# A grouped-expert decoder kernel: an earlier gate matrix, and a gather that leaves out padding rows

## The chip, the cores and the metric

The kernel runs on one core of one Trainium2 chip. The metric is the device time of one execution in microseconds (us), as the median of the runs. The engines are named as in the profile: PE is TensorE (PEld its weight loads), DVE is VectorE, ACT is ScalarE, POOL is GpSimd, SP is the engine that issues most DMAs. L671 is line 671 of the kernel.

## The reference

Two decoder layers over 512 tokens of width 1024, all in float32. Each layer has a mixer (sliding-window attention and a chunked mLSTM, gated, summed, one output projection) and then a grouped mixture of experts, which is where the change acts:

```python
h2 = rms_norm(x, norm_ffn_w[l]) * (1.0 + sc2) + sh2
x = x + g2 * grouped_moe(h2, router_w, router_bias, w_gate[l], w_up[l], w_down[l])
...
# grouped_moe: best of 4 groups, then the top 2 of its 4 experts; 16 experts in all
order = jnp.argsort(flat_e)
...
x_pad = jnp.zeros((n_blocks * MOE_BLOCK, D), xt.dtype).at[dest].set(xt[tok_sorted])
...
return (jax.nn.silu(xb @ w_gate[e]) * (xb @ w_up[e])) @ w_down[e]
```

Every token goes to two experts, so a layer has 1024 rows to work on. An expert has a gate and an up matrix of 1024x512 and a down matrix of 512x1024, 2 MB each. How many rows of the blocks below are real follows from the inputs; counted with the reference's router, 64 rows to a block, they are:

| layer | real rows of its blocks, in order | blocks |
|---|---|---|
| first | 64, 25, 64, 4, 47, 64, 38, 45, 64, 8, 54, 47, 64, 32, 63, 56, 63, 64, 8, 38, 63, 49 | 0 to 21 |
| second | 50, 34, 46, 52, 52, 64, 6, 64, 26, 64, 2, 64, 64, 10, 64, 13, 64, 16, 64, 39, 52, 23, 33, 58 | 0 to 23 |

## The kernel before, in words

The kernel is written engine by engine, with semaphores by hand. One loop over the two layers stands in each engine's program, and the order of the work is the order of the lines.

**The expert stage.** The 1024 rows are sorted by expert and cut into blocks of 64 rows; an expert's last block is filled up with padding rows. For each block PE transposes the 64 gathered rows (`x_transposes`, L1324), DVE and ACT scale them into feature layout (L1934, L920), PE multiplies them by the gate and up matrices (`gate_up`, L1332, 32 matmuls), ACT applies silu (L925), DVE multiplies the two halves (L1984, the product), PE transposes the hidden rows (L1338), ACT copies them (L928) and PE multiplies by the down matrix (`down`, L1344, 16 matmuls). The loop is software pipelined: in one pass PE runs the gate/up group of block b+1, the row transposes of block b+2, the down group of block b and the hidden-row transposes of block b+1. The loop's first pass is preceded by `x_transposes(0)`, `gate_up(0)`, `x_transposes(1)` and `h_transposes(0)`.

**Where the rows come from.** ACT stores the normalised token rows to a DRAM buffer, `token_rows` (L912). Block 0 is not gathered; it is picked on PE by one-hot matmuls (L1319, semaphore `first_rows`) and copied into the buffer `xg[0]` by ACT and DVE (L916, L1923). All later blocks are gathered by an indirect DMA that POOL issues (`gather_rows`, L671) into `xg[0]` or `xg[1]` in turn; these are the upper and lower 64 partitions of the first 1024 columns of `merged`, which the mixer's output projection read before. The list of token numbers, `idx`, is made on DVE and PE: one-hot matrices of row in block, block, and token tile (L1920 to L1929), a matmul that sums them (L1368), and two DVE instructions that join tile and row to a token number (L1941, L1942). A padding row finds no token, so its sum is 0 and it gathers token 0. POOL issues the gather for block 1 as soon as `idx` is there, and the gather for block b+2 when the transposes of block b are done. The loop also issues one gather past the last block.

**Where the weights lie and when they are loaded.** There are three buffers for each of gate, up and down; expert e uses buffer e mod 3. All loads go through SP, in this order before the expert loop: the gate matrix of expert 1 (L554), up 0 (L557), down 0 and down 1 (L559, L560), gate 0 (L562), then after the output projection up 1 and down 2 (L564, L565), then gate 2 (L567) and up 2 (L570). Gate 2 goes into `hT`, the mixer's feature buffer. The mixer's last matmul from it is over before L559, but its first two 512-column slices also serve as the place where ACT writes squares that nobody reads (`squares`, L146; L906, only the row sums count); so SP waits for the four square passes (`ffn_sq`, L566) before it loads gate 2. Up 2 goes into `regA`, where the normalised rows lie until block 0 is picked and the rows are stored; so SP waits for `first_rows` and `rows_out` (L568, L569). Then SP issues the small parameter loads of the next layer (first layer only), waits until all engines have reached the expert stage, clears the mixer's semaphores, and loads each further expert when its buffers come free: gate and up behind the last gate/up group of expert e-3, down behind its last down group (`load_expert`).

**What else lies on the path.** On POOL the lines before the first gather are L674 to L676: the wait for the cleared semaphores, for the stored rows, and for `idx`. `vaug` is the mLSTM's value buffer, 2064 columns wide and free in the expert stage; its first 1024 columns hold a quarter of the second expert's down matrix.

## Time and profile before

| | us |
|---|---|
| runs, median (three: 1625.84, 1629.93, 1628.45) | 1628.45 |
| the profiled execution | 1632.27 |
| its span, first to last instruction | 1630.5 |
| PE busy in it | 1525.3 |
| DVE busy | 671.4 |
| ACT busy | 325.2 |
| POOL busy | 127.6 |

The profiled execution is 3.82 us above the median of the runs, and 1.77 us of it lie around the span. How to read the rows further below: a page's chain gives the shares of the span along the chain of work that ended last. The chain in order of time gives start, length and what it was. A timeline row gives start, length, engine, line, operation, output<-input, shape and count, and in brackets how long the engine was idle before it and what ended that. A row by stretch gives from:to, its length, the busy time of PE, PEld, DVE, ACT and POOL with instructions in brackets, the granted TensorE clock as a share of full speed, the busy share of the DMA engines and GB/s.

### The profile page before, as it was taken

Reading aid. Unit: us, or ns where it says so; the run is one execution under the profiler, and the core shown is the slowest. Engines: PE = TensorE matmul, PEld = TensorE weight load, DVE = VectorE, ACT = ScalarE, POOL = GpSimd, SP = SyncE. Lnnn points to the kernel's source line nnn. Section 1 sums busy time; section 2 is a strip of 40 time slices with the busy share of each in tenths; the row PEclk is TensorE's granted clock in tenths of the full one; section 3 lists DMA queues with packets and bytes.
Section 4 is the critical chain, followed back from the end, with each engine's and each line's share of the span. In section 5 each row is a group of like instructions: output and inputs, shape, how many; then the busy total and the mean of one; then the engine's idle time right before and its main releaser. Section 6 shows DMA issues by size and latency. Waiting matters only on the chain.

```text
span 1630.5 us, 19269 instructions
## 1 busy us (share of the span) xinstructions
PE 1525.3 (94%) x6035; PEld 690.6 (42%) x6036; DVE 671.4 (41%) x1670; ACT 325.2 (20%) x836; POOL 127.6 (8%) x197
## 2 busy tenths in 40 slices
PE   5999999989998899989889999999899988999996
PEld 2644445544454333323354444454444533333332
DVE  1446425557625322211345554365673351212224
ACT  3234411100001212111143342111000111212120
POOL 1100000001000010100110000000100010101001
PEclk9999999999999999999999999999999999999998
DMA  9961112377726799999954012126765389997895
GB/s 337 347 243 52 52 52 100 107 258 268 282 81 244 219 354 389 390 387 393 346 193 176 1 52 103 52 103 210 288 225 218 107 315 390 392 383 254 317 346 200
DMA packets 131893, 376.10 MB, mean 231 GB/s; under 512 B 12232, under 2 KB 14448, under 8 KB 131824
## 3 DMA queue, kind: packets, MB, share of 16 engines
q1 hardware_dynamic: 117440, 337.51, 55.9%
q0 software_dynamic: 5984, 20.45, 4.0%
q10 hardware_dynamic: 8400, 17.31, 2.8%
q8 instruction: 33, 0.54, 0.1%
q14 instruction: 36, 0.29, 0.1%
HBM read 345.36 MB, written 29.88 MB: 230 GB/s over the span
## 4 chain that ended last, share of the span: by engine, by line
PE 80%; DMA 7%; DVE 5%; ACT 2%; issue 2%; SPq 1%; another core or an unknown queue 1%; POOL 0%; DVEq 0%; ACTq 0%; POOLq 0%
PE bank L1085 25%; PE bank L1332 17%; PE bank L1074 11%; PE bank L1344 8%; PE bank L1290 7%; DMA weight_ring<-in_w_up_dram 3%; DMA regA<-in_w_up_dram 2%; PE bank L1324 2%; DMA h_features<-in_ada_w_dram 1%; DMA merged_features<-token_rows,regU 1%; PE bank L1154 1%; PE bank L1338 1%; PE bank L1143 1%; DVE x_tokens L2033 1%
## 5 line engine op out<-in xcount | busy, mean ns | idle before, releaser
L1085 PE MATMUL bank<-h_features,weight_ring 128*128 128x512 f32 x768 | 344.0, 602 | 1.9 <-ACT regB L800 1.9
L1332 PE MATMUL bank<-weight_ring,merged_features 128*64 128x512 f32 x960 | 222.5, 618 | 14.8 <-DMA weight_ring<-in_w_up_dram 8.7
L1085 PEld LDWEIGHTS bank<-h_features,weight_ring 128*128 128x128 f32 x768 | 146.4, 193 | 183.3 <-issue 183.0
L1074 PE MATMUL bank<-weight_ring,h_features 128*128 128x512 f32 (+1 forms) x512 | 196.8, 541 | 5.0 <-ACT merged_features L760 3.8
L1984 DVE TENSOR_TENSOR merged_features<-bank,merged_features 64x512 f32<-64x512 f32 x46 | 31.9, 693 | 350.6 <-ACT merged_features L925 345.8
L1074 PEld LDWEIGHTS bank<-weight_ring,h_features 128*128 128x128 f32 x512 | 95.7, 190 | 99.4 <-issue 94.7
L1332 PEld LDWEIGHTS bank<-weight_ring,merged_features 128*64 128x64 f32 x960 | 73.0, 142 | 140.4 <-issue 136.6
L1344 PE MATMUL bank<-weight_ring,merged_features 128*64 128x512 f32 x528 | 122.3, 605 | 4.9 <-ACT merged_features L928 4.9
L1332 PE MATMUL bank<-h_features,merged_features 128*64 128x512 f32 x256 | 117.3, 612 | 8.0 <-DMA regA<-in_w_up_dram 6.9
L1290 PE MATMUL bank<-weight_ring,merged_features 128*128 128x512 f32 x256 | 116.3, 610 | 3.0 <-POOL merged_features L664 3.0
L1332 PE MATMUL bank<-regA,merged_features 128*64 128x512 f32 x256 | 117.7, 614 | 0.0
L925 ACT ACTIVATE merged_features<-bank 64x512 f32<-64x512 f32 x46 | 27.1, 589 | 330.2 <-PE bank L1332 330.2
L1290 PEld LDWEIGHTS bank<-weight_ring,merged_features 128*128 128x128 f32 x256 | 48.8, 195 | 59.9 <-issue 56.7
L1981 DVE TENSOR_TENSOR merged_features<-bank,g_rows 128x512 f32<-128x512 f32 x46 | 31.8, 691 | 86.2 <-PE bank L1344 82.5
L1332 PEld LDWEIGHTS bank<-h_features,merged_features 128*64 128x64 f32 x256 | 34.8, 141 | 70.8 <-issue 70.8
L920 ACT ACTIVATE merged_features<-bank,mod_cols,scale 128x64 f32<-128x64 f32 x192 | 62.0, 403 | 9.3 <-PE bank L1324 7.1
L1344 PEld LDWEIGHTS bank<-weight_ring,merged_features 128*64 128x64 f32 x528 | 35.9, 138 | 64.6 <-issue 62.5
L1085 PE MATMUL bank<-regB,weight_ring 128*128 128x512 f32 x128 | 57.9, 595 | 1.6 <-DVE regB L1784 1.6
L1085 PE MATMUL bank<-regA,weight_ring 128*128 128x512 f32 x128 | 57.7, 594 | 0.0
L1934 DVE TENSOR_SCALAR merged_features<-bank,scale,mod_cols 128x64 f32<-128x64 f32 x192 | 52.8, 336 | 4.2 <-PE bank L1324 2.0
L671 POOL DMA_INDIRECT merged_features<-token_rows,regU x46 | 43.9, 953 | 66.4 <-DVEq L1943 31.8
L642 POOL TENSOR_TENSOR fin_small<-fin_small,minus_half 128x4 f32<-128x4 f32 x8 | 8.1, 1007 | 509.3 <-DVEq L1533 509.3
(363 smaller groups left out, 1567.3 us busy)
## 6 DMA issues: line engine op xcount, KB each, us to landing
weight_ring<-in_w_gate_dram SPq DMA_DIRECT2D x22, 2048.0 KB
weight_ring<-in_w_up_dram SPq DMA_DIRECT2D x22, 2048.0 KB
weight_ring<-in_w_down_dram SPq DMA_DIRECT2D x22, 2048.0 KB, 16.6
weight_ring<-in_w_in_dram SPq DMA_DIRECT2D x18, 2048.0 KB, 13.7
x_tokens<-in_ada_w_dram SPq DMA_DIRECT2D x14, 2048.0 KB, 8.0
h_features<-in_w_gate_dram SPq DMA_DIRECT2D x10, 2048.0 KB
regA<-in_w_up_dram SPq DMA_DIRECT2D x10, 2048.0 KB
regA<-in_ada_w_dram SPq DMA_DIRECT2D x8, 2048.0 KB, 8.3
```

The lines of the kernel that those rows point to most:

```text
L671: po.indirect_dma_start(out=xg[p], out_offset=None, in_=xlin, in_offset=bass.IndirectOffsetOnAxis(ap=index, axis=0)).then_inc(xg_in[p], 16)
L920: last = ac.activation(xT[:, k, :], ps[2][:, MB * k:MB * k + MB], ACT.Identity, scale=A2[:, k:k + 1], bias=modc[:, 24 + k:25 + k])
L925: ac.activation(hsil[64:P, :], ps[3][0:64, :], ACT.Silu).then_inc(sil_ready, 1)
L1074: ins = te.matmul(bank[:, 0:w], hT[:, k, P * i:P * i + P], wv[:, k, :], start=(k == 0), stop=(k == KD - 1))
L1085: ins = te.matmul(bank[:, :], wv[:, k, c0:c0 + P], rhs[:, k, :], start=(k == 0), stop=(k == kn - 1))
L1290: ins = te.matmul(bank[:, :], merged[:, k, P * i:P * i + P], slot(f"wo{k // 4}", 4, D)[:, k % 4, 512 * h:512 * h + 512], start=(k == 0), s ...
L1324: ins = te.transpose(ps[(2, 6)[k % 2]][:, MB * k:MB * k + MB], xg[p][:, P * k:P * k + P], ident[MB * p:MB * p + MB, MB * p:MB * p + MB])
L1332: ins = te.matmul(ps[3][64 * part:64 * part + 64, :], xT[:, k, :], w[:, k, :], start=(k == 0), stop=(k == KD - 1))
L1344: ins = te.matmul(ps[5][64 * half:64 * half + 64, :], hxT[:, k, :], down_w[p][k][:, 512 * half:512 * half + 512], start=(k == 0), stop=(k ...
L1934: last = ve.tensor_scalar(xT[:, k, :], ps[6][:, MB * k:MB * k + MB], A2[:, k:k + 1], modc[:, 24 + k:25 + k], ALU.mult, ALU.add)
L1981: ve.tensor_tensor(to, ps[5][:, :], g2bc[:, :], ALU.mult).then_inc(y_taken, 1)
L1984: ve.tensor_tensor(hx, ps[3][64:P, :], hsil[64:P, :], ALU.mult).then_inc(hx_ready, 1)
```

## The change

It has two parts. SP issues the gate matrix of the third expert (expert 2) ahead of the first down matrices and no longer waits for the square passes; for that, the squares' scratch moves from `hT` to columns 1024 to 2047 of `vaug`. And the list of token numbers is shifted so that a padding row gets 1024 where it got 0: the tile number is counted from -8 (`iog` holds -8 to -5) and 8 x 128 = 1024 is added again at the end, so that a real row's number comes out as before while a row without a token keeps 1024. The gather gets a bound of 511 and leaves out rows beyond it without an error. A left-out row keeps what its buffer held; therefore POOL clears `xg[1]` once per layer, behind the wait for the first expert's rows.

```diff
--- before.py
+++ after.py
@@ -143,7 +143,6 @@
         gate_parts = regU[:, 519:519 + S]
         mflat = merged[:, :, :].rearrange("p a b -> p (a b)")
         small = mflat[:, 0:D]
-        squares = hT[:, 0:2, :].rearrange("p a b -> p (a b)")
         head_squares = mflat[:, 1024:2048]
 
         xg = [mflat[0:MB, 0:D], mflat[MB:2 * MB, 0:D]]
@@ -160,6 +159,7 @@
 
         zeros = vaug[:, :, :, :].rearrange("p a b c -> p (a b c)")[:, 0:D]
         vflat = vaug[:, :, :, :].rearrange("p a b c -> p (a b c)")
+        squares = vflat[:, D:2 * D]
         yg = [[regB[:, D * i:D * i + D] for i in range(NT - 1)] + [vflat[:, 0:D]], [xn[:, i, :] for i in range(NT)]]
 
         as8 = lambda ap: ap.rearrange("p (k n) -> p k n", k=KD)
@@ -303,6 +303,7 @@
         lg_taken = lsem("lg_taken")
         first_picked, first_rows, first_low, first_high = (lsem(n) for n in (
             "first_picked", "first_rows", "first_low", "first_high"))
+        rows_empty = lsem("rows_empty")
         z_there, inverse, idx_sum, idx_there = (lsem(n) for n in ("z_there", "inverse", "idx_sum", "idx_there"))
         routed, tables, combined = lsem("routed"), lsem("tables"), esem("combined")
         xt_ready, xt_evac_a, xt_evac_d, gu_ready, sil_ready, hx_ready, ht_ready, ht_evac, y_ready, y_taken = (
@@ -556,6 +557,7 @@
                 through(sp, "gb", 7)
                 load_up(0, 0)
                 through(sp, "yb", 7)
+                load_gate(2, 2)
                 load_down(0, 0)
                 load_down(1, 1)
                 summed(sp, len(STREAM) - 1)
@@ -563,8 +565,6 @@
                 through(sp, "wo", 2 * NT - 1)
                 load_up(1, 1)
                 load_down(2, 2)
-                sp.wait_ge(ffn_sq, NT)
-                load_gate(2, 2)
                 sp.wait_ge(first_rows, 1)
                 wait_reg(sp, rows_out, l * (16 * NT) + 16 * NT)
                 load_up(2, 2)
@@ -669,8 +669,12 @@
                 def gather_rows(p, index):
 
                     po.indirect_dma_start(out=xg[p], out_offset=None, in_=xlin,
-                                          in_offset=bass.IndirectOffsetOnAxis(ap=index, axis=0)).then_inc(xg_in[p], 16)
-
+                                          in_offset=bass.IndirectOffsetOnAxis(ap=index, axis=0),
+                                          bounds_check=S - 1, oob_is_err=False).then_inc(xg_in[p], 16)
+
+                pool.wait_ge(first_rows, 1)
+                po.memset(xg[1], 0.0).then_inc(rows_empty, 1)
+                pool.wait_ge(rows_empty, 1)
                 wait_reg(pool, moe_cleared, l + 1)
                 wait_reg(pool, rows_out, l * (16 * NT) + 16 * NT)
                 pool.wait_ge(idx_there, 1)
@@ -1925,7 +1929,7 @@
                 link(ve.tensor_tensor(at_block, io64[:, 0:32].unsqueeze(1).to_broadcast([P, 2 * NT, 32]),
                                       block.unsqueeze(2).to_broadcast([P, 2 * NT, 32]), ALU.is_equal))
                 link(ve.tensor_tensor(at_tile.rearrange("p (k i) b -> p k i b", k=2), at_block.rearrange("p (k i) b -> p k i b", k=2),
-                                      io64[:, 0:NT].unsqueeze(1).unsqueeze(3).to_broadcast([P, 2, NT, 32]), ALU.mult))
+                                      iog[:, :].unsqueeze(1).unsqueeze(3).to_broadcast([P, 2, NT, 32]), ALU.mult))
                 link(ve.tensor_scalar(at_block, at_block, pcol[:, 0:1], None, ALU.mult))
                 ve.sem_inc(inverse, 1)
 
@@ -1938,7 +1942,7 @@
                 dve.wait_ge(xt_ready, 1)
                 xt_dve()
                 dve.wait_ge(idx_sum, 1)
-                link(ve.tensor_copy(r(800, 32)[0:MB], ps[7][0:MB, P:P + 32]))
+                link(ve.tensor_scalar(r(800, 32)[0:MB], ps[7][0:MB, P:P + 32], 8.0 * P, None, ALU.add))
                 link(ve.scalar_tensor_tensor(idx[:, :], ps[7][0:MB, P + 32:P + 64], float(P), r(800, 32)[0:MB], ALU.mult, ALU.add))
                 ve.sem_inc(idx_there, 1)
 
```

## Rows read from the trace of the kernel before

**Rows 1.** The page's chain that ended last, whole span, by engine.

```profile
PE 80%; DMA 7%; DVE 5%; ACT 2%; issue 2%; SPq 1%; another core or an unknown queue 1%; POOL 0%; DVEq 0%; ACTq 0%; POOLq 0%
```

**Rows 2.** The chain in order of time: start, length, what it was.

```profile
523.67 8.84 DMA merged_features<-token_rows,regU
...
549.90 7.06 PE bank L1332 x32
...
706.53 27.39 DMA weight_ring<-in_w_up_dram
...
758.10 28.37 DMA weight_ring<-in_w_up_dram
...
1312.04 8.95 DMA merged_features<-token_rows,regU
...
1352.56 26.07 DMA regA<-in_w_up_dram
```

**Rows 3.** Engines, granted clock and DMA by stretch.

```profile
460.00:503.00 43.00, 42.21 (x148) 20.41 (x147) 11.35 (x20) 4.64 (x9) 1.11 (x2) 1.00 0.06 25
507.00:527.00 20.00, 15.96 (x109) 9.29 (x111) 15.66 (x70) 2.50 (x8) 2.06 (x2) 1.00 1.01 395
...
535.00:543.00 8.00, 7.72 (x24) 2.60 (x26) 5.11 (x22) 0.00 (x0) 0.71 (x1) 0.61 0.38 105
...
586.00:786.00 200.00, 189.82 (x958) 70.28 (x952) 39.73 (x96) 36.21 (x96) 16.57 (x30) 0.97 1.03 388
1339.00:1376.00 37.00, 34.66 (x180) 12.82 (x176) 7.46 (x18) 6.79 (x18) 3.33 (x6) 1.00 1.01 379
```

**Rows 4.** SP's queue: issues of gate 2, up 2, and down 3 in the second layer.

```profile
506.64 0.37 SPq L520 DMA_DIRECT2D h_features<-in_w_gate_dram  x1
519.96 0.37 SPq L523 DMA_DIRECT2D regA<-in_w_up_dram  x1
...
1338.33 0.37 SPq L527 DMA_DIRECT2D weight_ring<-in_w_down_dram  x1
```

**Rows 5.** The gather's line in 500 to 586, 586 to 786, and 1339 to 1376.

```profile
DMA to landing us min/median/max: 3.7/4.5/8.8
...
L671 POOL DMA_INDIRECT merged_features<-token_rows,regU x15: 927/927/930, 594.0 to 768.9; - x15
...
DMA to landing us min/median/max: 6.8/6.9/7.1
...
L671 POOL DMA_INDIRECT merged_features<-token_rows,regU x3: 932/932/935, 1347.9 to 1371.1; - x3
```

**Rows 6.** The timeline around the first gather of both layers.

```profile
523.67 1.51 POOL L671 DMA_INDIRECT merged_features<-token_rows,regU  x1 [15.93 <-DVEq L1943]
...
531.83 0.69 DVE L1984 TENSOR_TENSOR merged_features<-bank,merged_features 64x512 f32<-64x512 f32 x1 [2.54 <-issue]
...
532.64 0.49 PE L1324 MATMUL bank<-ident,merged_features 64*128 64x64 f32 x5 [2.45 <-DMA merged_features<-token_rows,regU]
532.91 0.27 PE L1338 MATMUL bank<-ident,merged_features 64*128 64x64 f32 x1
...
535.28 10.01 PE L1332 MATMUL bank<-weight_ring,merged_features 128*64 128x512 f32 x32 [1.91 <-ACT merged_features L920]
...
1319.95 0.69 DVE L1984 TENSOR_TENSOR merged_features<-bank,merged_features 64x512 f32<-64x512 f32 x1 [2.27 <-remote]
1321.13 0.49 PE L1324 MATMUL bank<-ident,merged_features 64*128 64x64 f32 x5 [2.55 <-DMA merged_features<-token_rows,regU]
...
1324.07 9.86 PE L1332 MATMUL bank<-weight_ring,merged_features 128*64 128x512 f32 x32 [2.20 <-ACT merged_features L920]
```

**Rows 7.** A memset on POOL, and two instructions of VectorE.

```profile
L613 POOL MEMSET mlstm_v_and_one<- 128x1024 f32 x1 | 0.9, 950 | 0.0
...
L1563 DVE TENSOR_SCALAR regP<-x_tokens,c_padded x8: 477/1531/1535, 344.9 to 1203.2; 128x512 f32<-128x512 f32 x8
...
520.36 0.41 DVE L1925 TENSOR_TENSOR regU<-iota,regP 128x256 bf16<-128x256 f32 x1
```

## The prediction, made before the changed kernel was run

> **What bounds the kernel now.** I read the page's chain first, then the chain in order of time, then the timeline around the two places where the change acts, then the DMA share by stretch.
>
> The chain [rows 1] names TensorE for 80% of the span and DMA for 7%. So a saving counts only where one of the few DMA links of that chain gets shorter, or where TensorE's own work moves closer together. The chain in time [rows 2] has these links. In each layer, TensorE waits once for the gather of the second block of expert rows (8.84 and 8.95 us from the issue on POOL to the landing). In the first layer it later waits twice for an up matrix that landed 27.39 and 28.37 us after its issue, the second time at the last expert; in the second layer once, 26.07 us after issue. A 2 MB matrix needs some 5.4 us at 388 GB/s, so those loads stood in a queue for most of that time. The stretches confirm it [rows 3]: from 586 to 786 us all DMA engines are busy (share 1.03, 388 GB/s), from 1339 to 1376 as well (1.01, 379 GB/s). From 460 to 503 us DMA is nearly idle (0.06), from 507 to 527 it is full (1.01).
>
> So there are two kinds of time to win: bytes that leave the two full stretches, and the wait for the first gather.
>
> **The gate matrix of the third expert.** Today it is issued at 506.64 and the up matrix of the same expert at 519.96 [rows 4], behind the up and down matrices of experts 1 and 2. The change issues the gate ahead of the first down matrices, before the idle stretch that begins at 460 [rows 3], so its 2 MB push the loads behind it back by some 5.4 us into that stretch. Those loads are first used once the first expert's rows are there, not before 519 us, so nothing waits for them. No DMA is added, and SP loses one wait. What it wins: TensorE waits for no weights in the next 180 us (the first such link of the chain is issued at 706.53 [rows 2]), so the earlier landing itself is worth 0. What it can help is the first gather, which today is issued (523.67) while up22, as I call the third expert's up matrix, is still queued behind the gate. up22 cannot be issued earlier (it overwrites the normalised rows), but it now meets an empty queue and ends near 526 (519.96 + 5.4), while today it is the last of a queue that is full to beyond 527 [rows 3]. In the first expert blocks a gather lands after 3.7 us at best, 4.5 in the middle and 8.8 for this one [rows 5]; I take 5 to 6.5 us, a landing 2.3 to 3.8 us earlier, before the first gate/up group ends at 530.19 (the 2.45 us of idle before 532.64 [rows 6]).
>
> How much of that reaches the end? In the first layer, the transposes of the gathered rows start at 532.64, and the transposes of the hidden rows at 532.91, right behind [rows 6]. The latter wait for VectorE's product, which starts at 531.83 after 2.54 us of its own issue (no data was late) and takes 0.69, so it ends at 532.52. That is what is late next: the wait moves from the gather to this product. The second gate/up group starts at 535.28, 2.4 us after the hidden-row transposes. Bounds for the gain: 0.1 us if that 2.4 us is TensorE's own queue (loop entry, expert numbers, branches), 1.0 us if it is only the scaling of the gathered rows, which VectorE could then start at 532.5. In the second layer the product ends at 1320.64, 0.5 us before the transposes start at 1321.13; there the bounds are 0.5 and 1.4. Both layers have nearly the same distance between the transposes and the next group (2.64 us from 532.64, 2.94 from 1321.13) and the same code, so I take the low ends: **0.15 and 0.5 us**.
>
> **The padding rows.** The reference's router gives 22 and 24 blocks of 64 rows, and each layer also gathers one block more than it has, all padding. In the full stretch of the first layer lie 15 gathers (issued 594.0 to 768.9 [rows 5]): blocks 8 to 21 and the empty one. Padding in them: 0, 56, 10, 17, 0, 32, 1, 8, 1, 0, 56, 26, 1, 15 and 64 rows, 287 in all. A padding row today is a 4 KB read like any other: the 15 land within 6.8 to 7.1 us, the empty one among them [rows 5]. Left out, they are 1.18 MB less; at 388 GB/s, **3.0 us**, and since the queue never runs dry there, the last expert's up matrix lands that much earlier and the layer ends that much earlier. In the full stretch of the second layer lie three gathers [rows 5], blocks 5, 6 and 7, with 0, 58 and 0 padding rows: 0.24 MB at 379 GB/s, **0.6 us**. Elsewhere the queue has idle time and the rows are worth 0. Bounds: 0 if a left-out row still costs a transfer, 3.6 if it costs none; I take 3.6, as a read that is not issued leaves the queue.
>
> **What is added.** One POOL memset of 64x1024 per layer, behind the wait for the first expert's rows and ahead of the first gather on POOL. A 128x1024 one took 0.95 us [rows 7]. Those rows are there just before 519.96, when SP issues up22 behind the same wait [rows 4], and POOL then idles until the gather at 523.67 [rows 6], so the memset is hidden with nearly 3 us to spare; without that cover each layer would lose 0.95. But it runs beside VectorE's index work, which lies on the path. The 128x512 VectorE scaling takes 0.477 us at its fastest and 1.53 as a rule [rows 7], so something holds it. I bound the price by 0 and 0.95 per layer; begun at about 519.8 the memset would still run for 0.35 us when L1925 is due (520.36 [rows 7]), and I take **0.35 us per layer**. The Trainium skill (GPSIMD Engine Reference, 8. Key points) says that GpSimd shares its SBUF interfaces with VectorE, with contention for instructions in a 2-port mode or with two SBUF inputs: L1925 would be one of these, and the full rule would give the upper bound, a sum of 2.4 instead of 3.6. The 1.53 us agrees with it; no row shows a memset beside VectorE.
>
> The index arithmetic keeps its instruction count and shapes, the scratch of the squares only changes its buffer: 0. The bounded gather has no row: its POOL time is bounded by 0.93 (today, median of the loop) below and, as nothing in the trace prices a check, left open above; in the loop it is covered by two blocks of matmuls.
>
> **Sum:** 0.15 + 0.5 + 3.0 + 0.6 - 2 x 0.35 = 3.55 us, taken as 3.6. The profiled execution took 1632.27 us (span 1630.5); it would take 1628.7. The median of the runs is 1628.45, 3.8 us lower, and all differences are local, so I predict 1628.45 - 3.6 = **1624.9**.
>
> **Rivals.** *A, the gap closes (faster).* If VectorE's scaling and not TensorE's queue sets the second group, it starts 1.0 and 1.4 us earlier. Its 32 matmuls now take 10.01 and 9.86 us against 7.06 a block later [rows 2, 6]: after the idle time the granted clock falls to its lower level of 1.2 GHz (mean 0.61 from 535 to 543 [rows 3]). A shorter gap may keep it at 2.4 GHz, worth 2.95 us in the first layer. In the second layer little of it counts: the down matrix of the fourth expert, issued at 1338.33 [rows 4], starts the full stretch, and the queue has only about 0.5 us of slack before it, which the 0.5 has used. Time: 1624.9 - 0.85 - 2.95 = 1621.1. For it: idle time there shrinks. Against it: the pause for VectorE's product remains.
> *B, left-out rows are not free.* If the descriptors are still made and drained, or the queue's share goes to nobody who is waited for, the 3.6 us stay: 1628.5. For it: nothing but that no row shows a skipped read.
> *C, slower: the bounded gather is slow on POOL.* The place is the first gather of each layer. It lands now at 532.50, and after the queue's relief there are some 3 us in hand before it sets the transposes again. At 0.1 us per row, 6.4 us more, it would be 3.4 us late in both layers: 1624.9 + 6.8 = 1631.7. From about 0.17 us per row one gather would outlast a block (15 in 174.9 us [rows 5], 12.5 us apart) and pace the whole loop. Against it: 0.93 us for 64 rows today is 15 ns per row.
>
> **Chances.** Forecast 0.62, A 0.20, B 0.11, C 0.07. No change means within 0.3% (4.9 us, 1623.6 to 1633.3), about what a measurement can tell. The forecast lies within it; a tenth of the chance, from its upper side, is beyond. Faster 0.20 + 0.10 = 0.30; slower 0.05 (C beyond 1633.3); the rest, 0.65, the same. The range takes in the forecast with its bounds, nearly all of A, and B: 1620.3 to 1629.4; C lies outside.
>
> **What would show it.** Right: no idle time of TensorE named for the first gather; VectorE's product named in its place before the second group; some 4.1 MB less on the software queue; the last up matrix of the first layer lands 3 us earlier relative to the start of its expert stage. Wrong: the gather landing is unchanged (then the queue ahead was not its delay); the second group runs in 7 us (A); the 15 gathers still land after 7 us and the full stretch is as long (B); POOL's gather instruction is several us long (C).

## The result, and the profile after

The changed kernel takes **1619.06 us** (median of 10 runs); beside it, on the same chip, the kernel before took 1625.96 (median of 10). The ratio is 0.995 with a 95% interval of 0.9937 to 0.9962: 6.9 us by the medians. Forecast were 1624.9 us and a gain of 3.6, so the time lies just below the range (1620.3). Part of the distance is the base: the three runs that the forecast started from had a median of 1628.45, ten have 1625.96. Timed again with the experiments, the change had a ratio of 0.9933 (0.9916 to 0.9951). So the gain is 7 to 10 us, two to three times the forecast.

Most lines of the changed kernel stand four below those of the kernel before (L1332 is now L1336); the gather is still L671.

The chain that ended last names DMA for 4% of the span, where it was 7% [rows 1]:

```profile
PE 82%; DVE 5%; DMA 4%; SPq 3%; ACT 3%; issue 2%; POOL 0%; DVEq 0%; ACTq 0%; POOLq 0%
```

The chain in order of time has no gather left in it, and the last up matrices land 26.14 and 23.29 us after their issue instead of 28.37 and 26.07 [rows 2]:

```profile
534.90 1.11 DVE merged_features L1938 x4
536.01 1.48 issue
537.49 7.09 PE bank L1336 x32
...
756.11 26.14 DMA weight_ring<-in_w_up_dram
...
1351.07 23.29 DMA regA<-in_w_up_dram
```

The timeline around the first gather of the first layer, answering to [rows 4, 6, 7] (the bracket at the end of a row is the engine's idle time and what ended it): SP issues the early gate matrix at 439.74 and the up matrix of the same expert at 521.59; the memset runs beside VectorE; TensorE starts the transposes of the gathered rows without a wait, and then waits for VectorE's product.

```profile
439.74 0.38 SPq L521 DMA_DIRECT2D h_features<-in_w_gate_dram  x1
...
521.40 0.95 POOL L676 MEMSET merged_features<- 64x1024 f32 x1 [12.03 <-PE bank L1323]
521.59 0.37 SPq L524 DMA_DIRECT2D regA<-in_w_up_dram  x1
521.99 0.41 DVE L1929 TENSOR_TENSOR regU<-iota,regP 128x256 bf16<-128x256 f32 x1
...
533.45 0.71 PE L1328 MATMUL bank<-ident,merged_features 64*128 64x64 f32 x8
534.17 0.69 DVE L1988 TENSOR_TENSOR merged_features<-bank,merged_features 64x512 f32<-64x512 f32 x1 [3.32 <-ACT merged_features L929]
535.01 0.43 PE L1342 MATMUL bank<-ident,merged_features 64*128 64x64 f32 x4 [0.86 <-DVE merged_features L1988]
```

The same two stretches of full DMA as in [rows 3]; the columns are busy time of PE, PEld, DVE, ACT and POOL with their instructions, then granted clock, DMA share, GB/s. The engines of the DMA are as busy as before, but move 391 and 390 GB/s instead of 388 and 379:

```profile
586.00:786.00 200.00, 189.90 (x964) 71.39 (x962) 39.75 (x96) 36.30 (x96) 17.16 (x30) 0.98 1.03 391
1339.00:1376.00 37.00, 34.69 (x180) 12.84 (x178) 7.46 (x18) 6.80 (x18) 3.44 (x6) 0.99 1.02 390
```

**How much of the two spans may be compared.** The span fell from 1630.5 to 1619.6, more than the medians. At the end of the second layer of the first profile stand two waits whose releaser the trace does not name:

```profile
1605.04 0.69 DVE L1981 TENSOR_TENSOR merged_features<-bank,g_rows 128x512 f32<-128x512 f32 x1 [3.53 <-remote]
1607.86 0.38 ACT L928 ACTIVATE merged_features<-bank 128x256 f32<-128x256 f32 x1 [6.88 <-remote]
```

They cost that execution 5.6 us (21.84 us from the last gate/up group to the matmuls of the kept rows); in all the 15 other profiles of this study, the unchanged kernel's second one among them, that stretch takes 16.24 us. It belongs to one execution and to neither kernel. The parts ahead of the experts, which the change hardly touches, also differ from profile to profile, by some 7 us, with the places where the granted clock falls. So the experiments are read by stretches that begin and end inside the expert stage:

- **S1**: from the gate/up group of block 15 to that of the last block in the first layer. It holds the second half of the first full DMA stretch, and its end is set by the last up matrix.
- **S2**: in the second layer, from SP's issue of the fourth expert's down matrix to the gate/up group of the sixth expert, which waits for an up matrix; **G** is how long that group then runs.

All from the timelines, in us; the time is the ratio to the kernel before in the same series, with its interval.

| kernel | ratio | S1 | S2 | G |
|---|---|---|---|---|
| before, first profile | | 84.78 | 40.44 | 9.82 |
| before, again | 0.9997 (0.9984 to 1.001) | 84.54 | 42.30 | 9.91 |
| early gate alone | 0.9985 (0.9971 to 1.0) | 84.35 | 40.43 | 9.69 |
| early gate alone, again | 0.9994 (0.998 to 1.0009) | 84.32 | 40.56 | 9.05 |
| the change, no row left out | 0.9977 (0.9964 to 0.999) | 84.88 | 40.40 | 9.20 |
| before, padding reads 64 rows | 1.0017 (1.0003 to 1.0032) | 84.49 | 40.36 | 9.64 |
| left out in blocks 1 to 7 | 0.9968 (0.9953 to 0.9982) | 84.29 | 38.85 | 8.78 |
| left out from block 8 on | 0.9963 (0.9949 to 0.9978) | 81.82 | 40.78 | 9.47 |
| left out in block 6 | one run | 85.06 | 37.63 | 8.78 |
| left out in blocks 9, 13, 18, 22 | one run | 81.68 | 40.54 | 9.51 |
| left out in blocks 8 to 21 but these | one run | 85.14 | 40.38 | 9.65 |
| rows left out, gate as before | 0.9932 (0.9913 to 0.995) | 81.21 | 37.88 | 8.78 |
| the same without memset | 0.9943 (0.9921 to 0.9964) | 81.40 | 37.88 | 8.78 |
| the change | 0.995 (0.9937 to 0.9962) | 81.27 | 37.64 | 8.78 |
| the change, again | 0.9933 (0.9916 to 0.9951) | 81.49 | 38.44 | 8.78 |
| the change without memset | 0.9939 (0.992 to 0.9959) | 81.54 | 37.48 | 8.78 |

(42.30 in the second line: there the fourth down matrix was issued 2.3 us earlier after the first pick than in the first profile, behind a queue that had not drained: the DMA engines were busy, at 405 GB/s, in the last 1 us before the issue, and moved 127 GB/s there in the first profile.)

### The profile page after: what moved, and what is told of

Its sections match the earlier page's. It is cut to its first block, busy times and chain, and to the rows that moved or that the text cites. A ratio compares the mean times of both kernels' runs of the same rounds, so it can differ in the third digit from the quotient of the medians.

```text
span 1619.6 us, 19319 instructions
## 1 busy us (share of the span) xinstructions
PE 1523.4 (94%) x6035; PEld 691.9 (43%) x6036; DVE 671.6 (41%) x1670; ACT 326.1 (20%) x836; POOL 131.6 (8%) x199
## 2 busy tenths in 40 slices
DMA packets 131893, 371.97 MB, mean 230 GB/s; under 512 B 13242, under 2 KB 15458, under 8 KB 131824
## 3 DMA queue, kind: packets, MB, share of 16 engines
q0 software_dynamic: 5984, 16.32, 3.2%
## 4 chain that ended last, share of the span: by engine, by line
PE 82%; DVE 5%; DMA 4%; SPq 3%; ACT 3%; issue 2%; POOL 0%; DVEq 0%; ACTq 0%; POOLq 0%
PE bank L1089 26%; PE bank L1336 18%; PE bank L1078 12%; PE bank L1348 8%; PE bank L1294 7%; DMA weight_ring<-in_w_up_dram 2%; PE bank L1328 2%; DMA regA<-in_w_up_dram 1%; DMA h_features<-in_ada_w_dram 1%; PE bank L1342 1%; PE bank L1158 1%; PE bank L1147 1%; DVE x_tokens L2037 1%; SPq L524 1%; DVE regP L1569 1%
## 5 line engine op out<-in xcount | busy, mean ns | idle before, releaser
L1336 PE MATMUL bank<-weight_ring,merged_features 128*64 128x512 f32 x960 | 222.0, 616 | 15.2 <-DMA weight_ring<-in_w_up_dram 8.9
L1336 PEld LDWEIGHTS bank<-weight_ring,merged_features 128*64 128x64 f32 x960 | 73.2, 141 | 140.2 <-issue 136.4
L1336 PE MATMUL bank<-h_features,merged_features 128*64 128x512 f32 x256 | 114.5, 601 | 4.2 <-DMA regA<-in_w_up_dram 3.2
L1336 PE MATMUL bank<-regA,merged_features 128*64 128x512 f32 x256 | 115.0, 603 | 0.0
L1336 PEld LDWEIGHTS bank<-h_features,merged_features 128*64 128x64 f32 x256 | 34.1, 138 | 64.6 <-issue 64.6
L671 POOL DMA_INDIRECT merged_features<-token_rows,regU x46 | 44.9, 976 | 44.3 <-POOL regU L688 19.5
```

Source lines behind the costliest of these rows:

```text
L671: po.indirect_dma_start(out=xg[p], out_offset=None, in_=xlin, in_offset=bass.IndirectOffsetOnAxis(ap=index, axis=0), bounds_check=S - 1, o ...
L1336: ins = te.matmul(ps[3][64 * part:64 * part + 64, :], xT[:, k, :], w[:, k, :], start=(k == 0), stop=(k == KD - 1))
```

## The experiments

**The two parts, each alone.** Rows alone, as an edit of the change (the scratch of the squares goes back to `hT` as well):

```diff
                 through(sp, "yb", 7)
-                load_gate(2, 2)
                 load_down(0, 0)
...
                 load_down(2, 2)
+                sp.wait_ge(ffn_sq, NT)
+                load_gate(2, 2)
```

> The part on padding rows alone: gate matrix of the third expert and the scratch of the squares as before; index 1024, bounded gather and memset as in the change. Theory (the bytes pay): most of the change's 6.9 us is here: 1620 to 1622 us, the last up matrix of the first layer lands 3 to 4 us earlier after the first pick than before, while TensorE still waits for the first gather, as it stands behind the same queue. Rival (the gate pays, by an earlier second gate/up group that keeps the clock): within 2 us of the kernel before, 1624 to 1627. Rival (the code after the expert loop): the two waits for an unknown releaser behind the last expert (6.88 and 3.53 us in the second layer) are there or not whatever the edit.

Gate alone, as an edit of the change (the two index operations are as before, too):

```diff
-                                          in_offset=bass.IndirectOffsetOnAxis(ap=index, axis=0),
-                                          bounds_check=S - 1, oob_is_err=False).then_inc(xg_in[p], 16)
+                                          in_offset=bass.IndirectOffsetOnAxis(ap=index, axis=0)).then_inc(xg_in[p], 16)
...
-                pool.wait_ge(first_rows, 1)
-                po.memset(xg[1], 0.0).then_inc(rows_empty, 1)
-                pool.wait_ge(rows_empty, 1)
```

> The early gate matrix alone: its load ahead of the first down matrices and the squares in the other scratch; gather without bound, padding index 0, no memset. Theory (the bytes pay): 1623.5 to 1625.5, the first gather lands 2 to 4 us earlier, the full stretch is as long as before. Rival (the gate pays): 1619 to 1621, the second gate/up group of the first layer runs in about 7.1 us instead of 10.

Measured: rows alone 1615.75 us against 1626.85, more than was expected of them; gate alone 1623.86, ratio 0.9985, inside what was expected if the bytes pay. Leaving out the rows shortens S1 and S2, the gate neither. The gate does what it was meant to do for the queue, but less than forecast: the up matrix of the third expert meets an idle queue and still lands 8.2 to 8.3 us after its issue in the first layer, and the first gather 7.67 us after its own (7.04 in the second profile, 8.84 before). In the first layer of the first of these profiles TensorE still waits for that gather:

```profile
537.64 0.68 PE L1323 MATMUL bank<-ident,merged_features 64*128 64x64 f32 x8 [1.28 <-DMA merged_features<-token_rows,regU]
```

The second rival fails: with the gate alone the second gate/up group of the first layer took 8.58 us, not 7.1.

**The kernel before, again.**

> The kernel before, unchanged, profiled again. If the waits for an unknown releaser behind the last expert belong to that program, they come back with 6.9 and 3.5 us within 0.5; if they are luck of one execution, they are shorter or gone, and the profiled span is some 4 to 6 us shorter than 1630.5. The time is that of the kernel before within 0.1%.

1625.83 us, span 1623.6; the two unnamed waits are gone. They were luck of one execution, and none of the change's gain.

**The bound without its effect** (padding index 0, everything else as in the change):

```diff
-                                      iog[:, :].unsqueeze(1).unsqueeze(3).to_broadcast([P, 2, NT, 32]), ALU.mult))
+                                      io64[:, 0:NT].unsqueeze(1).unsqueeze(3).to_broadcast([P, 2, NT, 32]), ALU.mult))
...
-                link(ve.tensor_scalar(r(800, 32)[0:MB], ps[7][0:MB, P:P + 32], 8.0 * P, None, ALU.add))
+                link(ve.tensor_copy(r(800, 32)[0:MB], ps[7][0:MB, P:P + 32]))
```

> The whole change but for the index: the two index operations on VectorE stay as before, so padding rows read row 0 again and the bound leaves none out; early gate, memset and bound check are in. It leaves out nothing of the result. Theory (the bytes pay): 1623.5 to 1625.5 as with the early gate alone, plus at most 0.7 for the memset. Rival (the bytes cost nothing, the rest pays): 1619 to 1620, as the whole change. The memset beside VectorE shows as a longer index operation, by at most 0.95 us a layer.

1624.17 us; S1 and S2 as before. Early gate, memset and bound check together are worth about as much as the gate alone. The last sentence of the expectation was wrong: L1929 took 0.41 us beside the memset, as it did without one [rows 7].

**One row read many times?** Before, all padding rows read row 0. This kernel reads 64 different rows instead, as many bytes:

```diff
+ link(ve.tensor_scalar(r(596, 1)[0:MB], pcol[0:MB, 0:1], -8.0, 8.0 * P, ALU.mult, ALU.add))
+ link(ve.tensor_scalar(r(564, 32)[0:MB], r(532, 32)[0:MB], 8.0 * P - 0.5, None, ALU.is_gt))
+ link(ve.tensor_scalar(r(564, 32)[0:MB], r(564, 32)[0:MB], r(596, 1)[0:MB], None, ALU.mult))
+ link(ve.tensor_tensor(idx[:, :], r(532, 32)[0:MB], r(564, 32)[0:MB], ALU.subtract))
```

> The kernel before, but a padding row r of a block reads token row 8r instead of row 0: as many bytes and packets as before, from 64 different rows. Four more tiny VectorE operations ahead of the first gather of a layer, some 0.7 us, of which the second gate/up group may wait for a part. Theory (the bytes pay): 1626 to 1628, not faster than before; in the second layer the up matrix of the sixth expert lands 40 to 41 us after the issue of the fourth down matrix, as before (40.4), and its 16 parts still lie 2 us apart from the median to the last. Rival (many reads of one row hold up one of the DMA engines, and the change wins by leaving that row alone): that landing comes after 38.5 to 39.5 us, with the last part within 1 us of the median, and the time falls by 2 us or more.

1629.01 us, S2 40.36: nothing is won by leaving row 0 alone. That rival falls. The time lies above the expected 1626 to 1628; the gap before the second gate/up group is 6.80 and 6.38 us there, behind the four added operations (5.09 and 5.49 before). One sign of the expectation was wrong: the 16 parts in which the matrix lands are 0.5 us apart from the middle one to the last, not 2. With the gate alone that distance is 2.0 in one profile and 0.8 in the other, with the last part at the same place, so it is no measure of the padding.

**Which blocks?** The index is shifted for some columns of the list only, one column to a block; the first of the two kernels:

```diff
+ link(ve.tensor_tensor(at_tile.rearrange("p (k i) b -> p k i b", k=2)[:, :, :, 0:8],
+                      at_block.rearrange("p (k i) b -> p k i b", k=2)[:, :, :, 0:8],
+                      iog[:, :].unsqueeze(1).unsqueeze(3).to_broadcast([P, 2, NT, 8]), ALU.mult))
+ link(ve.tensor_tensor(at_tile.rearrange("p (k i) b -> p k i b", k=2)[:, :, :, 8:32],
+                      at_block.rearrange("p (k i) b -> p k i b", k=2)[:, :, :, 8:32],
+                      io64[:, 0:NT].unsqueeze(1).unsqueeze(3).to_broadcast([P, 2, NT, 24]), ALU.mult))
...
+ link(ve.tensor_copy(r(800, 32)[0:MB], ps[7][0:MB, P:P + 32]))
+ link(ve.tensor_scalar(r(800, 32)[0:MB, 0:8], ps[7][0:MB, P + 0:P + 8], 8.0 * P, None, ALU.add))
```

> The whole change, but only the padding rows of blocks 1 to 7 get index 1024; those of later blocks read row 0 again. One or two more VectorE operations ahead of the first gather. Theory (bytes in the full stretches pay): the first layer's full stretch (blocks 8 to 21) is as long as before, 84.4 us from the gate/up group of block 15 to that of the last block; in the second layer the up matrix of the sixth expert lands 37.5 to 38 us after the issue of the fourth down matrix (40.4 before); 1621 to 1623 in all. Rival (the rows of the first layer are all that pays): both stretches as before, 1624.

> The counterpart: only the padding rows of blocks 8 and later are left out. Theory (bytes in the full stretches pay): 81.2 us from the gate/up group of block 15 to that of the last block in the first layer (84.5 before), 40.4 in the second layer as before; 1620 to 1622 in all. Rival (the gain comes from the few blocks of the second layer's start): 1624.

1621.82 and 1622.21 us. The first shortens S2 and leaves S1, the second S1 and leaves S2, so both layers pay, each through its own full stretch; either half is worth 4 to 5 us with the gate. S2 in the first, 38.85, is longer than the 37.5 to 38 that were expected; the experiment on block 6 alone shows why.

**The change again.**

> The change itself again, with a profile. Theory: 1617 to 1621; 81.2 us in the first layer's full stretch and 37.6 us to the up matrix of the sixth expert in the second, as in the first profile of it; the place and number of the low stretches of the granted clock differ, and so do the parts in front of the experts, by 2 or 3 us either way. If its stretches differ from the first profile of it by as much as from the kernel before, nothing can be read from single profiles.

1616.99 us, S1 81.49, S2 38.44: the stretches repeat within some 0.2 and 0.8 us.

**The memset, the gate, once more.** The change, and rows alone, without the memset, and the gate alone a second time:

```diff
-                pool.wait_ge(first_rows, 1)
-                po.memset(xg[1], 0.0).then_inc(rows_empty, 1)
-                pool.wait_ge(rows_empty, 1)
```

> The change without its memset and the two waits around it: rows that the first gather leaves out keep what the buffer held, finite numbers that no token reads. Theory (the memset's price is off the path: the first gather is issued 0.6 us later with it, but TensorE does not wait for that gather): the same as the change within 1 us, 1616 to 1619; first gather issued 7.6 us after the first pick's start instead of 8.2. Rival (0.35 to 0.6 us a layer are on the path): faster than the change by 0.7 to 1.2 us.

> The part on padding rows alone, without the memset: the gate matrix is loaded where it was before. Theory (left-out bytes carry the gain): 1615 to 1619, no slower than the change; 81.2 us from the gate/up group of block 15 to the last one in the first layer, 37.6 to 38.6 us from the issue of the fourth down matrix to the gate/up group of the sixth expert in the second. Rival (the early gate matrix carries 2 to 3 us of the change): 1619 to 1621.

> The early gate matrix alone, again, for a tighter interval: by the idle time that it takes out of the path (0.04 us in each layer in the first profile of it) the same as before within 0.1%; by its first timing 0.15% faster. TensorE names VectorE's product and not the gather ahead of the second gate/up group in both layers.

1616.26, 1617.93 and 1624.63 us (ratios 0.9939, 0.9943, 0.9994). The memset costs nothing that these runs can tell; the gate adds nothing where rows are left out (0.9932 and 0.9943 without it, 0.995, 0.9933 and 0.9939 with it). One reason in the expectation was wrong. The first gather is indeed issued 8.24 us after the first pick's start instead of 7.63, but it is so without the memset too. The index list is complete at 524.93 in the profile of the change (L1946 ends) and the gather starts at 525.91; before, these were 523.30 and 523.67. So the bounded form itself starts 0.6 us later, while the loop's gathers are hardly longer (0.967 us, 0.927 before [rows 5]).

**Block 6 alone.** The same edit with column 6 as the only shifted one (`[:, :, :, 6:7]`). The expectation set the engine time of 58 rows against a hold-up of the whole queue.

> The change with only block 6's padding rows left out: 58 in the second layer, 26 in the first. Theory (a left-out row is worth its engine time, some 0.24 us on one of 16 engines, 0.9 us for 58 rows): in the second layer 39.3 to 39.7 us from the issue of the fourth down matrix to the gate/up group of the sixth expert (40.4 with none left out, 38.9 with blocks 1 to 7). Rival (the gather of block 6 held the queue up as a whole): 38.9 or less. The first layer's full stretch as before, 84.4.

S2 is 37.63: **the whole gain of S2 comes from leaving out rows of this one gather**, 2.8 us where its 58 rows are 0.6 by their bytes. Here the theory of the forecast falls. The next two views say why. First, 4 us of the kernel before and of this one, both begun 3.5 us after the issue of block 6's gather (columns as above):

```profile
1362.90:1366.90 4.00, 4.00 (x22) 1.47 (x20) 0.00 (x0) 0.00 (x0) 0.00 (x0) 1.00 1.04 341
```

```profile
1360.50:1364.50 4.00, 4.00 (x22) 1.43 (x20) 0.00 (x0) 0.00 (x0) 0.00 (x0) 1.00 1.03 405
```

All 16 DMA engines are busy in both (1.04, 1.03), but while 64 rows are gathered they move 341 GB/s, and 405 while six are. The 4 us after such a gather show 416 GB/s or so; after block 5's, in the kernel before:

```profile
1354.80:1358.80 4.00, 4.00 (x26) 1.50 (x23) 0.64 (x1) 1.30 (x4) 0.18 (x1) 1.00 1.04 416
```

So a gather of 64 rows takes its 0.26 MB, 0.64 us at 410 GB/s, and on top of that (410 - 341) x 4 = 0.28 MB of what the queue would have moved, 0.67 us. Second, the queues over S2, the kernel before and the change (queue, packets, MB, share of 16 engines):

```profile
q1 hardware_dynamic: 3346, 13.24, 87.3%
q0 software_dynamic: 287, 0.91, 7.9%
```

```profile
q1 hardware_dynamic: 3286, 13.00, 89.5%
...
q0 software_dynamic: 220, 0.44, 4.1%
```

The gathers are q0. It falls by 0.47 MB, and block 6's padding is only 0.24 of them. The rest is the gather of block 7: before, it was issued at 1371.1 and its rows came ahead of the awaited up matrix (1378.63); now that matrix lands at 1374.36, 4.6 us after the gather's issue at 1369.7, and most of the rows come behind it. By these rates one emptied gather gives some 1.2 us, and that lets the next one slip behind the transfer that is waited for, up to another 1.3.

The profiles can be put in order by it. In the kernels that leave block 6 whole, all 64 rows of block 7 begin ahead of the sixth expert's group. With blocks 1 to 7 left out, 62 of them still do, and S2 is 38.85: the emptied gather by itself is worth 1.6 us. In the others that empty it, 47, 30, 28, 19, 14 and 8 rows do, and S2 is 38.44, 37.88, 37.88, 37.64, 37.63 and 37.48. So what the second step adds differs from execution to execution, 0.4 to 1.4 us; no run moved the gather of block 7 by itself.

**Does the same hold in the first layer?** There the forecast in bytes had come out right (3.0; S1 fell by 3.2). The four emptiest gathers of the full stretch alone, and the thinned ones alone; the first of the two kernels (the constant 1024 is added for the same columns):

```diff
+ link(ve.tensor_tensor(at_tile.rearrange("p (k i) b -> p k i b", k=2)[:, :, :, 0:32],
+                      at_block.rearrange("p (k i) b -> p k i b", k=2)[:, :, :, 0:32],
+                      io64[:, 0:NT].unsqueeze(1).unsqueeze(3).to_broadcast([P, 2, NT, 32]), ALU.mult))
+ link(ve.tensor_tensor(at_tile.rearrange("p (k i) b -> p k i b", k=2)[:, :, :, 9:14:4],
+                      at_block.rearrange("p (k i) b -> p k i b", k=2)[:, :, :, 9:14:4],
+                      iog[:, :].unsqueeze(1).unsqueeze(3).to_broadcast([P, 2, NT, 2]), ALU.mult))
+ link(ve.tensor_tensor(at_tile.rearrange("p (k i) b -> p k i b", k=2)[:, :, :, 18:23:4],
+                      at_block.rearrange("p (k i) b -> p k i b", k=2)[:, :, :, 18:23:4],
+                      iog[:, :].unsqueeze(1).unsqueeze(3).to_broadcast([P, 2, NT, 2]), ALU.mult))
```

> The change with padding rows left out in blocks 9, 13, 18 and 22 alone: 56, 32, 56 and 64 rows, 208 of the 287 in the first layer's full stretch. More small VectorE operations ahead of the first gather, which shift the start of the experts and not the stretch that is read. Theory D (a gather costs its bytes and, for some 4 us, a part of the rate of the whole queue, and only one that is mostly empty gives the rate back): the stretch from the gate/up group of block 15 to that of the last block as short as with all left out, 81.0 to 81.6 us. Theory B (each left-out row is worth 4 KB at 388 GB/s, 10.6 ns): 84.5 - 2.2 = 82.3.

> The counterpart: left out in blocks 8 to 21 but for 9, 13 and 18: 79 rows in eight gathers that keep 38 to 63 of their 64 rows. Theory D: nothing, 84.3 to 84.9 us. Theory B: 84.5 - 0.8 = 83.7.

81.68 and 85.14 us: theory D. The 208 rows of four gathers carry 2.9 of the 3.2 us, the 79 rows of eight others show no gain (one profile each; the kernels that leave out no row of S1 lie between 84.29 and 85.06). The same windows of 4 us in both, first the emptiest alone, for the gathers of blocks 17 (full), 18 (8 rows), 21 (full) and 22 (none):

```profile
709.80:713.80 4.00, 4.00 (x20) 1.41 (x18) 0.00 (x0) 0.00 (x0) 0.00 (x0) 1.00 1.03 345
721.40:725.40 4.00, 4.00 (x20) 1.55 (x18) 0.00 (x0) 0.00 (x0) 0.00 (x0) 1.00 1.03 395
...
765.10:769.10 4.00, 4.00 (x20) 1.36 (x18) 0.00 (x0) 0.00 (x0) 0.00 (x0) 1.00 1.03 334
776.70:780.70 4.00, 4.00 (x22) 1.70 (x20) 0.00 (x0) 0.00 (x0) 0.00 (x0) 1.00 1.03 404
```

then the thinned ones alone, for the gathers of blocks 18 (full), 19 (38 rows), 21 (49) and 22 (full):

```profile
720.10:724.10 4.00, 1.69 (x6) 0.83 (x8) 0.00 (x0) 0.00 (x0) 0.00 (x0) 0.84 1.03 334
736.80:740.80 4.00, 0.77 (x2) 0.33 (x4) 0.00 (x0) 0.00 (x0) 0.00 (x0) 0.89 1.03 346
766.00:770.00 4.00, 4.00 (x20) 1.35 (x18) 0.00 (x0) 0.00 (x0) 0.00 (x0) 1.00 1.04 324
777.60:781.60 4.00, 4.00 (x22) 1.70 (x20) 0.00 (x0) 0.00 (x0) 0.00 (x0) 1.00 1.03 342
```

A gather of 8 or no rows gives the rate back (395, 404), one of 49 runs at 324 although it moves a quarter less itself. All 16 profiles say the same. In the 4 us that begin 3.5 us after the issue, for blocks 8 to 22 of the first layer and 5 to 7 of the second, the engines move 334 GB/s in the mean (289 to 352) with 64 rows, 327 (291 to 349) with 38 to 56, 373 (364 to 380) with 32, and 392 (362 to 406) with 8 or fewer; in the next 4 us it is 414.

A rival to the rate is left in part. A matrix lands in 16 parts, and the wait ends with the last of them. For the last up matrix of the first layer the first and the last lie 0.5 to 0.7 us apart where no row of S1 is left out, 1.65 with the thinned gathers alone, 1.05 with the emptiest alone, and 2.2 to 2.5 with all of them. So leaving out rows brings the parts forward unequally, and the last one least. With the thinned gathers alone the middle part comes no earlier either (84.5 us from block 15's group, 83.8 to 84.3 in the six kernels that leave out nothing), so this is not the whole reason; the runs do not separate its share. (The times of these two, 1630.15 and 1631.1 in one run each, hold more VectorE work ahead of the first gather and are not used.)

## Why the prediction was wrong, step by step

**The gate matrix (0.15 + 0.5): the direction right, the relief smaller, the size not shown.** The up matrix behind the gate was to end 5.4 us after its issue and the gather to land after 5 to 6.5, before the first gate/up group ends. With the gate alone the matrix took 8.2 to 9.3 us, and the gather 7.67 and 7.04 in the first layer and 6.12 and 5.88 in the second. In the first layer of one of these profiles TensorE still waits for it for 1.28 us, and for 2.50 with the bound and the memset added. In the change it lands after 5.79 and 4.97, where rows of block 1 are left out too, and no idle time of TensorE is named for it. VectorE's product is what is late next, as forecast, though not for its own issue: in most profiles it waits for ACT's silu. From the end of the first gate/up group to the start of the second the first layer has 4.95 us with the gate alone against 4.99 and 5.09, and 4.87 with rows left out and the gate as before. The second layer, in executions whose first group ran at the full clock (7.09 us), has 4.93 against 5.49, one execution each; where that group took 8.78, it is 4.2 with the gate and without, since the gather then cost little or nothing. The timings of the gate alone, 0.9985 and 0.9994, agree with little or nothing.

**The padding rows of the first layer (3.0): right in sum, by another price.** S1 falls from 84.6 (mean of the six kernels that leave no row out) to 81.4 (mean of the five that leave out all), 3.2 us. But it is not 287 rows at 4 KB each; it is four gathers, one half empty and three nearly so, at some 0.7 to 0.8 us. (By the window rates these four would give some 3.8 us, an estimate; the last part of the matrix came 2.9 earlier with them alone. That difference is not explained.) That the two prices agree in sum is chance: 56, 32, 56 and 64 rows are most of the 287.

**The padding rows of the second layer (0.6): the step that failed.** "In the full stretch of the second layer lie three gathers [...] 0.24 MB at 379 GB/s" priced them by bytes, and "3.6 if it costs none" was taken for an upper bound of the whole. S2 falls by 2.6 (40.44 to 37.86, means of the five kernels on each side; the 42.30 is left out): 1.6 of it is the emptied gather, and the rest the gather behind it, of which more now comes after the awaited matrix. The row that could have warned stands in [rows 3]: 379 and 388 GB/s are means over stretches that hold gathers, while between two gathers the same engines move some 414 (416 in the row of 1354.80). A mean rate prices the bytes of the mixture; it does not price what one part of it takes from the other.

**What came on top, and was not in the sum: the group behind the shorter wait.** The sixth expert's gate/up group runs 8.78 us in every kernel that leaves out block 6's rows, and 9.05 to 9.91 in the others. TensorE had waited 2.31 us for its matrix instead of 5.10; these are the wait and the group of the kernel before, then of the change:

```profile
1373.60:1378.60 5.00, 0.06 (x2) 0.00 (x0) 0.51 (x1) 0.38 (x1) 0.00 (x0) 0.89 1.03 344
1378.80:1388.60 9.80, 9.80 (x33) 3.16 (x34) 0.00 (x0) 0.00 (x0) 0.00 (x0) 0.72 1.03 412
```

```profile
1372.10:1374.40 2.30, 0.08 (x2) 0.00 (x0) 0.53 (x1) 0.38 (x1) 0.00 (x0) 1.00 1.06 411
1374.50:1383.30 8.80, 8.80 (x33) 3.23 (x34) 0.00 (x0) 0.00 (x0) 0.00 (x0) 0.81 1.02 382
```

The granted clock had begun to fall in the longer wait, and its mean over the group is 0.72 against 0.81 (between 1.2 and 2.4 GHz): 0.8 us by the means of G. The forecast had this mechanism in rival A, at another place.

**What was added (-0.7): nothing that the runs can tell.** The memset's VectorE price is 0. The bounded gather's later issue may reach the second group of the first layer (5.12 us of gap with it and the gate, 4.95 with the gate alone), by 0.2 us at most. The contention that the Trainium skill (GPSIMD Engine Reference, 8. Key points) states for two SBUF inputs does not show here: L1929, of that kind, overlapped the memset for 0.36 us, began 4.32 us after the start of the first pick and took 0.41, both as before.

**The sum as measured:** 3.2 + 2.6 + 0.8 + 0 to 0.5 = 6.6 to 7.1 us, less 0.2 at most, against 6.9 in the first series and 9.8 in the second. The five kernels with all rows left out lie 6.9 to 11.1 us below their reference, 8.8 on average, so some 2 us are not located: the last group of the first layer took 7.09 us in two of them and 8.4 or more in every kernel that leaves no row out, but no stretch shows a steady difference beyond the terms above. That stays open.

**The rivals.** A (second gate/up group faster): its time, 1621.1, was the nearest, but not its reason. That group ran in 7.09 us in the change, yet the first one then took 8.78 instead of 7.09; together 15.87, against 17.10 in the first profile of the kernel before and 15.51 in its second. B (left-out rows not free) is refuted as a whole, but half true in an unexpected way: a left-out row still makes a packet, of 4 bytes, and rows left out of a gather that stays mostly full showed no gain. C (bounded gather slow on POOL) fell: 0.967 us a gather.

## What to carry to other kernels

Where a queue is full, price a transfer by what it takes from the others: read the total rate in the few microseconds in which it runs and in those beside it, not the mean of the stretch. Here a gather in the full queue costs about twice its bytes by these rates, one that is nearly empty gives most of that back, and thinning gathers a little gave nothing in the one run that did only this. And count what the saved time lets slip behind the transfer that is waited for, and the clock of the work behind that wait.

## What the hardware showed unexpectedly

- A gather of 64 rows of 4 KB lowers what all DMA engines move together from 414 to some 334 GB/s for 4 us, though their busy share stays at 1.02 to 1.07. With 38 to 56 of the 64 rows it is no better (327 in the mean; 309 for the 47 rows of block 11 in the change, 310 for the 56 of block 15 in the kernel of the thinned gathers); with 8 or fewer it is 362 (block 9) to 406. Why a thinned gather holds the others up as long as a full one, no view shows.
- The rows that a bounded gather leaves out still make a packet each, but an empty one: the software queue has the same number of packets in the whole span (5984) and moves 16.32 MB instead of 20.45. 1010 packets more are under 512 bytes (13242 against 12232), as many as the padding rows that were gathered before, and each moves 4 bytes instead of 4096. The bounded form starts 0.6 us later after its index list (0.97 against 0.36 us).
- Whether the padding rows read one row or 64 different ones made no difference to S1 and S2.
- Single executions differ by waits that the trace does not name (5.6 us at the end of one) and by where the granted clock falls; two profiles should not be subtracted before one of them was taken twice.
